# Second block's difference attention: meta values in 128 rows, and the value product in natural layout

## The reference, cut to what matters

```python
s1 = einsum('bhqd,bhkd->bhqk', q1, k1) * scale - slope * dist
s2 = einsum('bhqd,bhkd->bhqk', q2, k2) * scale - slope * dist
a = softmax(s1) - lam * softmax(s2)
o = einsum('bhqk,bhkd->bhqd', a, v)
o = rmsnorm(o, sub_g) * (1.0 - lambda_init)      # over the 128 columns of one head
yb = o * silu(gb)
```

## Time and profile before

| | us |
|---|---|
| median of three runs | 2002.17 |
| the profiled execution | 2001.94 |
| its span in the trace | 2000.2 |
| PE busy (share of the span) | 1945.5 (97%) |
| DVE busy | 1146.7 (57%) |
| ACT busy | 888.1 (44%) |
| POOL busy | 200.3 (10%) |

### The profile page before, as it was taken

The page is one execution under the profiler, slowest core; times in us unless marked ns, Lnnn a source line. Parts: engine busy times, 40 slices in busy tenths (PEclk is TensorE's granted clock), DMA queues, the critical chain, the costliest instruction groups (busy, mean ns, idle before and its releaser), DMA issues.

```text
span 2000.2 us, 34078 instructions
## 1 busy us (share of the span) xinstructions
PE 1945.5 (97%) x13547; PEld 1787.2 (89%) x13547; DVE 1146.7 (57%) x1220; ACT 888.1 (44%) x1142; POOL 200.3 (10%) x114
## 2 busy tenths in 40 slices
PE   6999999999999999999999999999999999979997
PEld 6989999898899988988998898899879998878976
DVE  5546877476545655454455445544655457787554
ACT  5533333356543445443443344344543335535443
POOL 2002433110000100100010010001000010042000
PEclk9999999999999999999999999999999999999999
DMA  7564555555565566666666665666555643333553
GB/s 231 171 188 141 167 166 159 172 179 145 148 206 193 184 210 185 193 194 193 191 189 198 186 195 190 192 196 191 180 168 169 178 138 116 106 106 110 165 188 127
DMA packets 175844, 345.33 MB, mean 173 GB/s; under 512 B 10800, under 2 KB 11008, under 8 KB 175184
## 3 DMA queue, kind: packets, MB, share of 16 engines
q1 hardware_dynamic: 173984, 337.75, 55.4%
q0 software_dynamic: 1728, 5.65, 1.1%
HBM read 341.26 MB, written 2.10 MB: 172 GB/s over the span
## 4 chain that ended last, share of the span: by engine, by line
PE 91%; DVE 5%; ACT 2%; issue 1%; POOL 0%; DMA 0%; POOLq 0%; DVEq 0%; ACTq 0%
PE ps L369 54%; PE ps L381 30%; DVE wlo L1066 2%; PE ps L439 1%; ACT whi L739 1%; DVE obr L1458 1%; DVE rs_hg L1202 1%; PE ps L656 0%; PE ps L496 0%; PE ps L626 0%; PE ps L486 0%; PE ps L397 0%; PE ps L644 0%; DVE qsq L1366 0%; PE ps L478 0%
## 5 line engine op out<-in xcount | busy, mean ns | idle before, releaser
L1066 DVE TENSOR_TENSOR wlo<-raw,whi 128x1024 fp32r<-128x1024 f32 x632 | 818.2, 1301 | 736.6 <-ACT whi L739 735.5
L739 ACT ACTIVATE whi<-raw 128x1024 fp32r<-128x1024 f32 x632 | 665.7, 1059 | 970.4 <-PE ps L369 620.9
L369 PE MATMUL ps<-xhi,whi 128*128 128x256 f32 (+1 forms) x1984 | 576.3, 290 | 10.8 <-issue 3.9
L369 PE MATMUL ps<-xhi,wlo 128*128 128x256 f32 (+1 forms) x1984 | 563.4, 284 | 0.0
L369 PE MATMUL ps<-xlo,whi 128*128 128x256 f32 (+1 forms) x1984 | 563.2, 284 | 0.0
L369 PEld LDWEIGHTS ps<-xhi,whi 128*128 128x128 f32 x1984 | 379.8, 191 | 25.7 <-issue 19.8
L369 PEld LDWEIGHTS ps<-xlo,whi 128*128 128x128 f32 x1984 | 379.5, 191 | 1.9 <-issue 1.0
L369 PEld LDWEIGHTS ps<-xhi,wlo 128*128 128x128 f32 x1984 | 378.9, 191 | 0.0
L369 PE MATMUL ps<-x2hi,whi 128*128 128x256 f32 x1024 | 283.1, 276 | 1.1 <-issue 1.1
L369 PE MATMUL ps<-x2lo,whi 128*128 128x256 f32 x1024 | 283.0, 276 | 0.0
L369 PE MATMUL ps<-x2hi,wlo 128*128 128x256 f32 x1024 | 283.0, 276 | 0.0
(11 more groups left out here) (320 smaller groups left out, 2283.0 us busy)
## 6 DMA issues: line engine op xcount, KB each, us to landing
raw<-in_w_in_dram SPq DMA_DIRECT2D x280, 512.0 KB, 3.8
raw<-in_w_up_dram SPq DMA_DIRECT2D x128, 512.0 KB, 3.8
raw<-in_w_down_dram SPq DMA_DIRECT2D x128, 512.0 KB, 3.9
raw<-in_w_out_dram SPq DMA_DIRECT2D x64, 512.0 KB, 4.1
raw<-in_w_branch_a_dram SPq DMA_DIRECT2D x16, 512.0 KB, 5.2
raw<-in_w_branch_b_dram SPq DMA_DIRECT2D x16, 512.0 KB, 4.1
x_nat<-in_x_dram SPq DMA_DIRECT2D x4, 512.0 KB, 5.8
rel<-in_rel_bias_dram POOLq DMA_DIRECT2D x8, 256.0 KB, 4.0
```

Of the source, the lines that this page charges most:

```text
L369: ins = mm(outs[b], w[:, k % SLOTS, j, cols], v[:, kt, 0:n], start=start, stop=last and j == CK - 1 and i == 2, skip_group_check=True)
L739: f(whi[:, k % SLOTS], raw[:, k % SLOTS], ACT.Copy).then_inc(whi_ready, 1)
L1066: tt(wlo[:, k % SLOTS], raw[:, k % SLOTS], whi[:, k % SLOTS], ALU.subtract).then_inc(wlo_ready, 1)
```

## The change

- `v_meta` gets 128 rows, set to zero by POOL once before the meta rows are copied in; the third product of all 32 units runs over 128 rows. The third transpose of the weights covers columns 256 to 383 of the probability buffer instead of 256 to 271, and one ACT copy of 384 columns takes the place of two.
- For the difference heads the operands of the product are swapped, so that the queries are on the partitions (`o_nat`). The scaling of the first softmax by its own sum is left out, and the second is scaled by lambda times the ratio of the sums. The norm that follows divides a factor per row out again; its small constant is scaled with the squared sum.
- ACT squares each finished unit and sums its rows (`unit_squares`, positions 5 to 20). `b_norm` on DVE, positions 22 to 26, works out 128 x 16 factors, with a root on ACT at position 22 between, and scales `o_nat` in two halves. PE turns the 16 blocks back (`b_turn`, positions 24 and 25); ACT and DVE copy them to `ob`.
- POOL's squares and its multiplication by the reciprocal are gone; PE's products with ones, ACT's four roots and DVE's four large reciprocals are gone.

```diff
-POS_BN = 23
+POS_BN = 24
@@ PE
                     if u == B_UNITS:
-                        pe.wait_ge(bn_sd, 4)
+                        pe.wait_ge(bn_copied[0], 1)
+                        pe.wait_ge(bn_copied[1], 1)
@@ PE, weights_turn and values
+                if u == B_UNITS:
+                    pe.wait_ge(bn_copied[0], 2)
+                    pe.wait_ge(bn_copied[1], 2)
-                p = p2[:, u % 4, 0, :]
-                nc.tensor.transpose(ps[:, 6, 0:P], p[:, 0:P], ident[:])
-                nc.tensor.transpose(ps[:, 6, P:T], p[:, P:T], ident[:])
-                nc.tensor.transpose(ps[0:META, 6, T:T + P], p[:, T:TM], ident[:]).then_inc(u_t, 1)
+                p = p2[:, u % 4].rearrange("p a c -> p (a c)")
+                for i in range(3):
+                    ins = nc.tensor.transpose(ps[:, 6, i * P:(i + 1) * P], p[:, i * P:(i + 1) * P], ident[:])
+                ins.then_inc(u_t, 1)
...
-                mm(ps[:, 7, 0:P], v_nat[:, vh, 0, :], pt2[:, u % 2, 0:P], start=True, stop=False)
-                mm(ps[:, 7, 0:P], v_nat[:, vh, 1, :], pt2[:, u % 2, P:T], start=False, stop=False)
-                mm(ps[:, 7, 0:P], v_meta[:, vh, :], pt2[0:META, u % 2, T:T + P], start=False,
-                   stop=True).then_inc(u_pv, 1)
-            def b_norm_squares():
-                pe.wait_ge(bn_o2, 1)
-                pe.wait_ge(u_o, B_UNITS)
-                for i in range(4):
-                    mm(ps[:, 4 + i, :], ones[:], ob2[:, 2 * i:2 * i + 2, :], start=True,
-                       stop=True).then_inc(bn_ss, 1)
+                parts = (v_nat[:, vh, 0, :], v_nat[:, vh, 1, :], v_meta[:, vh, :])
+                for i, v in enumerate(parts):
+                    w = pt2[:, u % 2, i * P:(i + 1) * P]
+                    l, r = (w, v) if u < B_UNITS else (v, w)
+                    ins = mm(ps[:, 7, 0:P], l, r, start=i == 0, stop=i == 2)
+                ins.then_inc(u_pv, 1)
+            def b_turn(i):
+                if i == 0:
+                    pe.wait_ge(u_nm, B_UNITS)
+                    pe.wait_ge(u_pt, B_UNITS)
+                    pe.wait_ge(u_o, B_UNITS)
+                pe.wait_ge(bn_n, i + 1)
+                for u in range(8 * i, 8 * i + 8):
+                    ins = nc.tensor.transpose(ps[:, 4 + u // 4, (u % 4) * P:(u % 4 + 1) * P], o_nat[:, u, :], ident[:])
+                ins.then_inc(bn_t, 1)
@@ PE, side
-                if pos == POS_BN:
-                    b_norm_squares()
+                if pos in (POS_BN, POS_BN + 1):
+                    b_turn(pos - POS_BN)
@@ ACT
-                f(pt2[:, u % 2, 0:T], ps[:, 6, 0:T], ACT.Copy)
-                f(pt2[0:META, u % 2, T:T + P], ps[0:META, 6, T:T + P], ACT.Copy).then_inc(u_pt, 1)
+                f(pt2[:, u % 2, :], ps[:, 6, 0:3 * P], ACT.Copy).then_inc(u_pt, 1)
+            def unit_squares(u):
+                act.wait_ge(u_o, u + 1)
+                f(ob[:, u // 2, (u % 2) * P:(u % 2 + 1) * P], o_nat[:, u, :], ACT.Square, accum_out=ss_b[:, u:u + 1]).then_inc(bn_ss, 1)
@@ ACT, side
-                if POS_BN < pos <= POS_BN + 4:
+                if 0 <= pos - 5 < B_UNITS:
+                    unit_squares(pos - 5)
+                if pos == POS_BN - 2:
+                    act.wait_ge(bn_ms, 1)
+                    f(rn_b[:], rn_b[:], ACT.Sqrt, scale=1.0 / P).then_inc(bn_sd, 1)
+                if pos in (POS_BN + 1, POS_BN + 2):
                     i = pos - POS_BN - 1
-                    act.wait_ge(bn_ss, i + 1)
-                    f(obr[:, 2 * i:2 * i + 2, :], ps[:, 4 + i, :].rearrange("p (x c) -> p x c", x=2), ACT.Sqrt,
-                      bias=eps_t[:], scale=1.0 / P).then_inc(bn_sd, 1)
+                    act.wait_ge(bn_t, i + 1)
+                    f(ob[:, 4 * i:4 * i + 2, :], ps[:, 4 + 2 * i, :].rearrange("p (x c) -> p x c", x=2),
+                      ACT.Copy).then_inc(bn_copied[0], 1)
@@ DVE, unit_norm
-                    own(nc.vector.reciprocal(ri, rsum[:, u % 4, :]))
-                    own(ts(ri[:, 1:2], ri[:, 1:2], lams[:, 5:6], None, ALU.mult))
-                    own(ts(p[:, 0], p[:, 0], ri[:, 0:1], None, ALU.mult))
+                    own(nc.vector.reciprocal(ri[:, 1:2], rsum[:, u % 4, 1:2]))
+                    own(stt(out=ri[:, 1:2], in0=ri[:, 1:2], scalar=rs_b[:, u:u + 1], in1=lams[:, 5:6], op0=ALU.mult,
+                            op1=ALU.mult))
@@ DVE
+            def b_norm(step):
+                if step == 0:
+                    dve.wait_ge(bn_ss, B_UNITS)
+                    own(tt(rn_b[:], rs_b[:], rs_b[:], ALU.mult))
+                    stt(out=rn_b[:], in0=rn_b[:], scalar=EPS * P, in1=ss_b[:], op0=ALU.mult,
+                        op1=ALU.add).then_inc(bn_ms, 1)
+                elif step < 3:
+                    if step == 1:
+                        dve.wait_ge(bn_sd, 1)
+                        own(nc.vector.reciprocal(rn_b[:], rn_b[:]))
+                    half = slice(8 * step - 8, 8 * step)
+                    tt(o_nat[:, half, :], o_nat[:, half, :], spread(rn_b[:, half], [1, 8], [0, P]),
+                       ALU.mult).then_inc(bn_n, 1)
+                else:
+                    i = step - 3
+                    dve.wait_ge(bn_t, i + 1)
+                    nc.vector.tensor_copy(ob[:, 4 * i + 2:4 * i + 4, :],
+                                          ps[:, 5 + 2 * i, :].rearrange("p (x c) -> p x c", x=2)).then_inc(bn_copied[1], 1)
@@ DVE, side
-                if POS_BN + 1 < pos <= POS_BN + 5:
-                    i = pos - POS_BN - 2
-                    dve.wait_ge(bn_sd, i + 1)
-                    nc.vector.reciprocal(obr[:, 2 * i:2 * i + 2, :], obr[:, 2 * i:2 * i + 2, :]).then_inc(bn_rs, 1)
+                if POS_BN - 2 <= pos <= POS_BN + 2:
+                    b_norm(pos - POS_BN + 2)
@@ POOL
+            pool.wait_ge(pe_done, C_IN2)
+            nc.gpsimd.memset(v_meta[:], 0.0).then_inc(vm_zero, 1)
             rope(0)
-            pool.wait_ge(u_o, B_UNITS)
-            tt(ob2[:], ob[:], ob[:], ALU.mult).then_inc(bn_o2, 1)
             rope(1)
             rope(2)
...
-                pool.wait_ge(bn_rs, 2 * (i + 1))
-                tt(v, v, obr[:, half, :], ALU.mult).then_inc(bn_n, 1)
-                pool.wait_ge(bn_n, i + 1)
+                pool.wait_ge(bn_copied[0], i + 1)
+                pool.wait_ge(bn_copied[1], i + 1)
```

More of the change, by code:

```diff
@@ L124, in program @@
         rinv = sb("rinv", [P, 4, 2])
+        rs_b = sb("rs_b", [P, B_UNITS])
+        ss_b = sb("ss_b", [P, B_UNITS])
+        rn_b = sb("rn_b", [P, B_UNITS])
         cos_t = sb("cos_t", [P, TM])
@@ L186, in program @@
         v_nat = at("v_nat", 17, [P, 10, NT, P])
-        v_meta = at("v_meta", 27, [META, 10, P])
+        v_meta = at("v_meta", 27, [P, 10, P])
         ka = at("ka", 48, [P, KV2, TM])
@@ L193, in program @@
         oa = at("oa", 60.0625, [P, H2, T])
+        o_nat = at("o_nat", 60.0625, [P, B_UNITS, P])
         ob = at("ob", 68.0625, [P, H2, T])
@@ L201, in program @@
         p2 = at("p2", 108.75, [P, 4, 2, TM])
-        ob2 = at("ob2", 0, [P, H2, T])
-        obr = at("obr", 8.5, [P, H2, T])
         yt_hi = [at("yt_a_hi", 17, [P, 8, T], F32R), at("yt_b_hi", 0, [P, 8, T], F32R)]
@@ L247, in program @@
             "u_s", "u_nm", "u_exp", "u_p", "u_t", "u_pt", "u_pv", "u_o")]
-        bn_o2, bn_ss, bn_sd, bn_rs, bn_n, bn_y, bn_hi, yb2_ready = [sem(n) for n in (
-            "bn_o2", "bn_ss", "bn_sd", "bn_rs", "bn_n", "bn_y", "bn_hi", "yb2_ready")]
+        bn_ss, bn_ms, bn_sd, bn_n, bn_t, bn_y, bn_hi, yb2_ready = [sem(n) for n in (
+            "bn_ss", "bn_ms", "bn_sd", "bn_n", "bn_t", "bn_y", "bn_hi", "yb2_ready")]
+        bn_copied = [sem("bn_copied_act"), sem("bn_copied_dve")]
+        vm_zero = sem("vm_zero")
         an_y, an_hi, ya2_ready = sem("an_y"), sem("an_hi"), sem("ya2_ready")
@@ L964, in values_copy @@
                 act.wait_ge(vt_t[1], b // 2 + 1)
+                act.wait_ge(vm_zero, 1)
                 f(v_nat[:, b, :, :], ps[:, 4 + b % 4, 0:T].rearrange("p (t c) -> p t c", t=2), ACT.Copy)
-                f(v_meta[:, b, :], ps[0:META, 4 + b % 4, T:T + P], ACT.Copy).then_inc(vt_c[1], 1)
+                f(v_meta[0:META, b, :], ps[0:META, 4 + b % 4, T:T + P], ACT.Copy).then_inc(vt_c[1], 1)
             def rope_root(n, s):
@@ L978, in unit_exp @@
                 if u < B_UNITS:
-                    for i in range(2):
+                    for i, total in enumerate((rs_b[:, u:u + 1], rsum[:, u % 4, 1:2])):
                         ins = f(p2[:, u % 4, i, :], p2[:, u % 4, i, :], ACT.Exp, bias=nm[:, u % 4, i:i + 1],
-                                scale=-1.0, accum_out=rsum[:, u % 4, i:i + 1])
+                                scale=-1.0, accum_out=total)
                 else:
@@ L1358, in values_copy @@
                 dve.wait_ge(vt_t[0], b // 2 + 1)
+                dve.wait_ge(vm_zero, 1)
                 nc.vector.tensor_copy(v_nat[:, b, :, :], ps[:, 4 + b % 4, 0:T].rearrange("p (t c) -> p t c", t=2))
```

(8 more changed lines are left out.)

## The result

The changed kernel takes **2019.7 us**, the median of five runs (2017.32 to 2021.48), against 2002.17 before: a ratio of 1.0077, with a 95% interval of 1.0062 to 1.0092. (The ratios with an interval are not the quotients of the two medians; the kernel before scatters by some 7 us from run to run.) It is slower, where the prediction said 1991.5. The profiled execution took 2017.32 us with a span of 2015.5, 15.3 more than before.

What follows compares the result with a forecast made beforehand. PE was taken to bound the kernel, busy 1945.5 of 2000.2 us. Gains of 7.0 (height), 1.2 (dropped scaling) and 2.5 (norm stage) made 10.7 us, giving 1991.5 us; range 1982 to 1998.

Steps and rivals of the forecast that it cites:

- All of the change lies between 1650 and 1880 us: Whole kernel: the change's effect on time was placed only in this stretch of the second block.
- rival 3: Norm's stall to position 32: PE's low clock does not return, stage 17 us longer, whole near 2011; chance 0.04.
- The product's height: Value products of 32 units: full-height third product saves 0.28 us (bounds 0.09 and 0.31), at 25 units 7.0 us.
- Rival 2: Value products: height is not the price, a unit saves 0.09 us at most; whole 1996 to 1998.5; chance 0.13.
- The stage between the attentions: End of chunk 23 to start of chunk 32: 43.6 us in place of 46.1, a gain of 2.5.
- rival 4: DVE's chain before position 32: longer than the counted 19.3 us, so the stage gives nothing; whole 1994; chance 0.13.
- The norm's stall: Position 24: PE waits 5.9 us (bounds 0.9 and 5.9) for DVE's first scaling, whose small steps wait for POOL.
- Rival 1: Position 24: norm in time, PE waits 0.9 to 3.9 us, clock holds; whole about 1986.5; chance 0.25.
- The clock: Behind the norm's stall: PE's clock falls, 5.4 us at half speed lose 2.7 us, absorbing position 25's 1.4 us wait.
- The stalls after it: Unit 16, before position 32: wait for its maximum falls from 6.48 to 0.3 us; the second stall stays, 4.5 us.
- POOL's zeroing: Near 1500 us: some 1 us on POOL, a hundred microseconds ahead of its use.
- The 1.2 us of dropped scaling: Difference attention, where PE's chain runs through DVE: dropped scaling of 0.36 us and its 0.04 wait count three times.

Runs made afterwards that it cites:

- e1: Kernel before plus an unused buffer of 192 bytes a partition where the change put its three small ones; 2030.8 us, ratio 1.0142.
- e2: Changed kernel with its three small buffers put into columns of a buffer no longer read, so no tile moves; 1992.91 us, ratio 0.9960.
- e13: Changed kernel with 64 unused bytes behind its three small buffers, making the shift 256 bytes; 1992.99 us, ratio 0.9941.
- e5: e2 with the third product of each unit back at 16 rows, all else of the change in place; 2000.18 us, ratio 0.9989.
- e7: e2 with the norm one position later (`POS_BN = 25`); 1992.51 us, ratio 0.9958.
- e10: e2 with the norm's small steps two positions earlier (DVE at 20, ACT's root at 21, first scaling at 22); 1992.15 us, ratio 0.9946.
- e14: e10 with DVE's second scaling also earlier, at position 23, ahead of the eviction L1402; 1991.51 us, ratio 0.9934.
- e3: Kernel before plus an unused buffer of 64 bytes a partition where the change put its small ones; 2023.13 us, ratio 1.0101.
- e4: Kernel before plus an unused buffer of 256 bytes a partition where the change put its small ones; 2002.09 us, ratio 1.0002.
- e8: Kernel before with only the two weight buffers moved by 64 bytes, other tiles keeping their address within 256; 2032.01 us, ratio 1.0161.
- e12: Kernel before with the weights and every tile behind them moved by 64 bytes together; 2002.77 us, ratio 0.9996.
- e9: e2 with the weights' rows staggered by 64 bytes each in both input projections, for a constant distance of -64; 2003.49 us, ratio 0.9998.

## Why the prediction was wrong, point by point

**The step that failed** is the sentence "All of the change lies between 1650 and 1880 us". The three buffers appear in the diff, and I costed them at nothing without naming them. By e1 and e2 they cost 27 to 29 us, in some 880 us of products that no line of the change touches. The sign of the result comes from this alone. No rival had it: rival 3, on the slower side, was about the clock, which came back, in the windows above, about 3.6 us after PE had resumed.

With the layout held still the change gives 1992.91 (e2) and 1992.99 (e13), where 1991.5 was forecast, and the rest of the working is near the runs in its sum. Some of that is luck, as several of its terms were off in opposite ways (the 10.7 us that the changed kernel's own trace shows also hold the slower output projection, 90.1 us for 88.9; e2 shows 11.5):

- **The product's height.** Taken: 0.28 us a unit, bounds 0.09 to 0.31. Measured: 0.34 by the chains of e5 and of the changed kernel, 7.3 to 7.4 us for all of it against 7.0. The number of units was off the other way: PE's chain runs through the products of 24 units in the kernel before and 22 in the changed one, not 25, and 22 x 0.34 is 7.5. The mechanism is shown, at both ends of the low product; the upper bound was a little low, since the two ends together cost 0.34 and not the 0.29 that I had read from single starts. Rival 2 (the height is not the price) has fallen. The Trainium skill's TensorEngine Tiling (Array Packing), section Key Properties, a drain at a change of tiling mode, agrees with e5; the rule of the Trainium skill's TensorE: Matmul & The Clock Gate, section Why this matters for your kernels, that a height of 32 takes the time of 128, would have given nothing for the padding, and e5 decides against it here: the low product, of 16 rows, cost more than the full one.
- **The stage between the attentions.** PE's chunk of position 24 is released at 1777.55 after a wait of 0.65 for DVE's L1397, which I had not foreseen, so the chunk before ended at 1776.9; the chunk of position 32 starts at 1820.8: 43.9 us against 43.6. Without the stall at the norm (5.36) and what the clock cost (1.8) it is 36.7, where the sum had 35.0; a shorter stall and a cheaper clock made up for it. Part of it is rival 4's mechanism, on a smaller scale: DVE's chain took 20.1 us (1799.79 to 1819.92) for 19.3, as a lower half beside POOL's L1665 took 2.52 for 1.16. The stage still gave 2.2 us, so that rival 4 as a whole has fallen.
- **The norm's stall.** 5.36 us against 5.9. L1475 took 2.37 us and ended with POOL's L1668, as forecast, and here the Trainium skill's SBUF — State Buffer, section Who interferes with whom, and the trace agree. L1476 was not held up (0.17 us); in its place the lower half of chunk 27 was (2.09 for 1.16). Two misses that cancel. Rival 1, the norm in time, has fallen, and e7, e10 and e14 show why an earlier norm hardly pays: the rotary squares are late as well.
- **The clock.** The half clock was to cost 2.7 us; turn and chunk behind the stall took 1.94 and 3.58 us for 0.88 and some 2.85, which is 1.8. The second scaling's wait disappeared in it, as forecast: its turn, at 1793.25, did not wait.
- **The stalls after it.** Forecast 0.3 and 4.5, measured 1.42 and 4.09.
- **POOL's zeroing** took 1.18 us at 1527.92 and delayed nobody; ACT's squares had their cover.
- **The 1.2 us of dropped scaling** was not measured by itself; with the stage's 2.5 it makes 3.7, where e5 shows 4.1 by its trace.

The chances were wrong in the same place: 0.04 for slower was the price of one mechanism I could think of, with nothing kept for a change of the layout that the diff shows in three lines.

## What to carry to other kernels

A buffer declared ahead of others is part of the change's cost: before pricing a diff, list which tiles move and by how much, and if products read them, compare the start-to-start time of an untouched stretch (matmuls counted in a window at full clock) in both profiles before explaining anything. Where a kernel is bound by PE and becomes slower or faster in code that nobody touched, pad the new buffers to a multiple of 256 bytes and run again. A low product between full ones costs time at its entry and exit (0.34 us here), so zero rows that make it full can pay; and a stall on a chain that several engines share mostly moves when one step is moved.

## What the runs showed of the hardware that I had not expected

- The spacing of fp32 products of 128 x 128 x 256 depends on the distance between the SBUF addresses of moving and stationary operand: 113 ns at -64 modulo 256, 118 to 120 at the other distances that were run, at full clock and with no wait in the profile (before, after, e1, e3, e4, e8, e12, e13). In the products of 512 columns, where `y` is stationary and the weights are moving, it is 229 ns at +64 (before), 232 to 233 at -128 (after, e1, e8) and 227 at 0 (e3), so there another distance is the best. The slowest layout run (e8) took 1.6% more than the kernel before.
- In these products no other distance gave the good pace, but -64 alone is not enough: in e12 one quarter of four, in e9 two of four ran at 117 ns at distance -64. The pace changed at the start of a quarter, after other work, and then held for the whole of it; in e12 the down-projection behind the slow quarter was slow as well (233 ns for 229). At distance -128 there are two paces in the same way, 118.7 and 120.0 ns, in turn from quarter to quarter in the changed kernel. What the second condition is was not found and stays open. The kernels with the weights and the moved region at their old places within 256 bytes (before, e2, e4 to e7, e10, e13, e14) kept the good pace in all four quarters. Each of these is one profiled execution; whether e12's slow quarter comes in all of its executions is not known.
- Moving the weights' rows to give the first projection the good distance throughout gained 3.9 us there, where 3456 products at 113 ns instead of a mean of 117.7 would have given 16, so addresses modulo 256 do not tell the whole there either.
